# Four slots instead of three for split weights in a two-block transformer kernel, with half the space for dynamic descriptors

## What is computed

```python
x = x + hybrid_mixer(rms_norm(x, norm_mix_g), w_in, ...)
x = x + memory_cross_attention(rms_norm(x, norm_xa_g), mem, ...)
x = x + swiglu(rms_norm(x, norm_ffn_g), w_gate_ffn, w_up_ffn, w_down_ffn)
x = rms_norm(x, final_g)
...
x = x + _mixer(_rms(x, norm_mix_g), lb, w_in, b_in, ..., out_g, w_out)
x = x + _conv_glu(_rms(x, norm_ffn_g), w_up, ffn_conv_w, ffn_conv_b, w_down)
```

## Time and profile before

| | value |
|---|---|
| median of three executions | 1623.43 us |
| the profiled execution, its own time | 1622.02 us |
| its span, first to last instruction | 1620.3 us |
| instructions in it | 23388 |
| VectorE busy | 1084.5 us (67%) |
| ScalarE busy | 804.8 us (50%) |
| GpSimd busy | 145.7 us (9%) |
| read from memory, written | 284.58 MB, 96.50 MB |

### The profile page before, as it was taken

One profiled execution on the slowest core, in us unless ns is written; L12 is line 12 of the kernel. 1 busy time (PEld: TensorE's weight loads), 2 busy tenths in 40 slices (PEclk: granted clock), 3 DMA queues, 4 the chain that ended last, 5 costly groups with the idle time before them and its releaser, 6 DMA issues. The chain is left out here.

```text
span 1620.3 us, 23388 instructions
## 1 busy us (share of the span) xinstructions
PE 1608.4 (99%) x9266; PEld 1368.5 (84%) x9266; DVE 1084.5 (67%) x1592; ACT 804.8 (50%) x1242; POOL 145.7 (9%) x173
## 2 busy tenths in 40 slices
PE   9999999999999999999999999999999999999999
PEld 7788878888888779999999977777767788998889
DVE  5346755555564458886886897667555688867886
ACT  5344333332454347654654665257674455544453
POOL 0001001122210001000000020312111200000000
PEclk9999999999999999999999999999999999999999
DMA  7653985968756954555557749531213564463235
GB/s 296 245 186 104 245 261 180 324 251 220 231 178 215 242 149 142 185 179 184 183 181 239 248 155 246 183 136 54 66 65 117 150 200 141 119 201 106 87 87 185
DMA packets 83644, 290.32 MB, mean 179 GB/s; under 512 B 9472, under 2 KB 11648, under 8 KB 76560
## 3 DMA queue, kind: packets, MB, share of 16 engines
q1 hardware_dynamic: 76464, 238.46, 42.9%
q0 software_dynamic: 6784, 49.84, 14.6%
q10 hardware_dynamic: 288, 0.54, 0.1%
HBM read 284.58 MB, written 96.50 MB: 235 GB/s over the span
## 5 line engine op out<-in xcount | busy, mean ns | idle before, releaser
L2042 DVE TENSOR_TENSOR WL<-raw,WH 128x1024 fp32r<-128x1024 f32 (+2 forms) x358 | 420.9, 1177 | 206.3 <-ACT WH L1260 195.1
L1260 ACT ACTIVATE WH<-raw 128x1024 fp32r<-128x1024 f32 (+3 forms) x360 | 361.0, 1005 | 250.1 <-PE pst L576 243.3
L576 PE MATMUL pst<-XH,WH 128*128 128x512 f32 x960 | 385.9, 402 | 1.0 <-DVE XL L2054 0.6
L576 PE MATMUL pst<-XH,WL 128*128 128x512 f32 x960 | 374.4, 390 | 0.0
L576 PE MATMUL pst<-XL,WH 128*128 128x512 f32 x960 | 374.0, 390 | 0.0
L576 PEld LDWEIGHTS pst<-XH,WH 128*128 128x128 f32 x960 | 180.2, 188 | 49.0 <-issue 11.5
L576 PEld LDWEIGHTS pst<-XH,WL 128*128 128x128 f32 x960 | 180.2, 188 | 38.5
L576 PEld LDWEIGHTS pst<-XL,WH 128*128 128x128 f32 x960 | 180.4, 188 | 38.0 <-issue 2.6
L576 PE MATMUL pst<-XCH,WH 128*128 128x256 f32 x616 | 174.6, 283 | 0.3 <-ACT pst L1260 0.2
L576 PE MATMUL pst<-XCL,WH 128*128 128x256 f32 x616 | 174.3, 283 | 0.0
L576 PE MATMUL pst<-XCH,WL 128*128 128x256 f32 x616 | 174.3, 283 | 0.0
(11 more groups left out here) (314 smaller groups left out, 2385.5 us busy)
## 6 DMA issues: line engine op xcount, KB each, us to landing
raw<-wst SPq DMA_DIRECT2D x191, 512.0 KB, 4.0
raw<-sums SPq DMA_DIRECT2D x120, 256.0 KB, 2.9
sums<-wup POOLq DMA_DIRECT2D x8, 2816.0 KB, 35.7
sums<-sums SPq DMA_DIRECT2D x32, 704.0 KB, 6.2
sums<-wd POOLq DMA_DIRECT2D x8, 2816.0 KB, 19.5
raw<-wup SPq DMA_DIRECT2D x66, 256.0 KB, 2.9
sums<-wup SPq DMA_DIRECT2D x16, 704.0 KB, 5.5
sums<-wd SPq DMA_DIRECT2D x16, 704.0 KB, 10.8
```

Source lines behind the costliest of these rows:

```text
L576: return nc.tensor.matmul(out, lhs, rhs, start=start, stop=stop, skip_group_check=more)
L1260: return nc.scalar.activation(out, in_, func, **kw)
L2042: vec.tensor_tensor(WL[:, i % NHL, 0:n], raw[:, i % NRAW, 0:n], WH[:, i % NHL, 0:n].bitcast(F32), ALU.subtract).then_inc(wl, 1)
```

## The change

```diff
@@ -20,7 +20,7 @@
 CH = 8
 NRAW = 5
 WARM = 12
-NHL = 3
+NHL = 4
 NEG = -1.0e30
 EPS = 1e-6
@@ -3396,7 +3396,7 @@
-    nc = bacc.Bacc("TRN2", target_bir_lowering=False, num_devices=1)
+    nc = bacc.Bacc("TRN2", target_bir_lowering=False, num_devices=1, dynamic_dma_scratch_size=8192)
```

## The result

| | before | changed |
|---|---|---|
| median of 5 runs, us | 1623.37 | 1633.09 |
| lowest to highest | 1622.13 to 1624.02 | 1631.60 to 1634.50 |
| profiled execution, its time | 1622.02 | 1632.71 |
| its span | 1620.3 | 1631.0 |
| mean granted clock of the TensorE | 0.999 | 0.996 |

The changed kernel is slower: ratio 1.0062 with an interval of 1.0050 to 1.0075, that is 9.7 us. The forecast was 1623.0 us and its range ended at 1627.0, so this is a miss.

A forecast was written before the change was run, and what follows sets the result against it. The TensorE, busy 1608.4 of 1620.3 us, was taken as the bound. Terms -0.4 + 0.1 - 0.2 + 0.1, the rest 0, gave -0.4 us: 1621.6 profiled, 1623.0 as median, range 1619.8 to 1627.0.

The forecast's parts named there:

- What bounds the kernel, and what the change does to the waits: Whole kernel: TensorE is the limit; awaited counts stay, so ScalarE's 243.3 us stay and only waits on WL can shrink.
- the faster rival: Whole kernel: slots were the limit, so the TensorE's waits shrink by 6.3 us, to 1617.1 us; chance 0.05.
- Part 1: TensorE's three waits on WL, 0.8 us, placed in the first network's last products: -0.4 us taken, plus 0.1 and -0.2.
- the extra width: Norm chain after the first network: a 1024-wide split replaces a 768-wide one, up to +0.3 us, +0.1 taken.
- Part 2: Start of the kernel: ScalarE's third split ahead of ZH runs in idle time; cost 0.
- Part 3: Second mixer, loads behind the store of X: late landing makes ScalarE wait 9.7 us, costing the TensorE 0.1; bounds 0 and 9.7.
- What is queued behind: Second mixer: ScalarE's exponentials and ucol 2 to 3 us late; VectorE's half of the second split ends near 1048.9.
- the cover is just used up: Second mixer near 1051.3, TensorE's sum of squares of X: ScalarE's 9.7 us of waits cost the TensorE only 0.1.
- 310.20 us: A like place for a late load, expected in time or 1 to 2 us late; bounds 0 and 3.0, 0 taken.
- Part 4: Four large dynamic transfers from 154.01: half the descriptor space still holds them; cost 0.
- The load wait reaches the TensorE: Split at 1036.93, decided by the second load landing after 1046.6: 1628.3 us, or 1636 at worst; chance 0.09.
- a wait of over 1 us on the TensorE between 1043 and 1060: Second mixer: a sign that would make the forecast wrong, as would GpSimd's issues spreading over 20 us.

The follow-up runs named there:

- the loads ahead: The changed kernel with three more loads, of chunks 238 to 240, issued ahead of the store of X: 1622.12 us, ratio 1.0002.
- the two that move chunk 238: The changed kernel with chunk 238's split one call later, on ScalarE and VectorE: 1622.26 us, ratio 1.0000; on VectorE only: 1622.63 us, ratio 1.0004.
- three-slot kernel: The kernel before, three slots and full space, with one load fewer (chunk 237) ahead of the store of X: 1630.83 us, ratio 1.0050.
- three splits held: Four slots, three more loads ahead of the store of X, splits of chunks 226, 254 and 262 one call later: 1623.38 us, ratio 1.0008.

## Why the prediction was wrong

**What bounds the kernel, and what the change does to the waits: right.** The awaited counts are the same, and ScalarE's waits for a slot stayed at 240.5 us of 243.3. The slots weren't the limit. With the loss taken away, four slots give a ratio of 1.0002 (0.9992 to 1.0011), which leaves out the 6.3 us of the faster rival.

**Part 1, the waits on WL: the row went as forecast, the term has the wrong sign.** The row is gone, and the wait for TL rose from 1.2 to 1.9 us. The step took half of the 0.8 us to stay and 0.1 for the extra width, -0.3 in all. It put all three waits at the end of the first network. Two of them, 0.4 us, stand there. The third stands in the second network of the kernel before, where nothing takes the gain back:

```profile
1282.78 0.47 PE L576 MATMUL pst<-XH,WH 128*128 128x512 f32 x1 [0.38 <-DVE WL L2042]
```

At the first place all that was gained went, and more. Between the same two TensorE instructions, at 930.1 and 972.98 in the kernel before, the four kernels with four slots and no split held there (the changed one, the loads ahead, and the two that move chunk 238) take 43.9 us, and the four kernels with three slots 42.9: a loss of 1.1 us. At 1282.78 each of the four gains 0.5. By these two places the term is about +0.5, outside the bounds that the step gave (-0.8 and +0.3). The spread of the runs is wider than that.

**Part 2, the extra split at the start: right.** ZH starts at 30.80 us where it started at 30.95.

**Part 3, a load that hasn't landed: the step that failed.** The right chunk, the right place in ScalarE's stream and the right wait were named: 6.5 us expected, 6.38 measured in the three-slot kernel and 8.39 in the changed one, where the load took 11.64 us and the store stood 0.8 us later. The total of waits on loads, 14.7 us for "some 15", agrees by luck: the first wait was 2 us longer than forecast, and the second, of "some 2 us", didn't come. What failed is the next sentence, "What is queued behind". It lists ScalarE's exponentials and ucol, and follows VectorE only for its half of the **second** split. VectorE's half of the **first** was left out. That one stands directly ahead of lines 2904 and 2905, whose sums the TensorE used 0.25 us after they were ready. So "the cover is just used up" was said of a place with cover, while 10 us earlier on another engine there was next to none. For the path that the step did follow, 0.1 us was not far off: with ScalarE alone late by 7.5 us the TensorE waited 0.7 us.

The right working from rows of the kernel before: the load lands at 1043.4 instead of in time for 1036.9. ScalarE's half, VectorE's half and the two additions take 1.04 + 1.2 + 0.8 us behind it, so the TensorE goes on at about 1046.5 instead of 1040.15. That is 6.3 us, and 1629.7 us in all. The three-slot kernel with one load late is this case: its TensorE lost 6.3 us at this place. Its loss of 8.8 us in all is larger by the clock's share. The bounds of the part, 0 to 9.7 us, held the 8.3 us that the TensorE lost at this place, but not the clock's share, which comes on top.

**What no term held: the clock.** A bottleneck that stands 6.1 or 8.1 us goes on at the lower level for about 5 us, and this cost 2.3 us after the longer stop and 2.2 after the shorter. The rest of the distance is the landing, 11.6 us instead of 9.7. The TensorE's 8.3 at the wait, 2.3 for the clock, and the 0.8 that it was behind before, less the 0.7 regained later, give the 10.7 us between the spans.

**310.20 us: right.** ScalarE's split there has no wait for its load.

**Part 4, the space: right.** 1622.3 us with the space alone, beside 1622.0.

**The rivals.** "The load wait reaches the TensorE" was the right one, with too small a chance, 0.09, and for a reason that doesn't hold: it was tied to the landing of the second load, as if only a late copy could decide it. The place that decides was the first split, and there the wait was certain from the order of instructions and a landing time already read. It had 1636 us only with a mishap at 310.20 added; the price that VectorE's stream gives for a landing in 9.7 us is 1629.7, and 1631.9 with the clock's 2.2. The rest of the measured 1633.09 is in the main the later landing. What was to show the forecast wrong, "a wait of over 1 us on the TensorE between 1043 and 1060", came at 1049.28.

## What to carry to other kernels

A wait that is put into an in-order stream is paid by everything behind it on that engine, and when a step is computed in halves on two engines, each half has its own queue behind it. List for every engine that takes part the next instruction that the bottleneck needs, and its room: here 0.25 us on VectorE and some 7 us on ScalarE. A deeper prefetch whose compute runs one step further ahead needs loads that go out one step earlier too. If a store or another wait holds the loads back in their queue, the prefetch moves a wait for memory forward into the path. The cost of each of the two stops of the TensorE was more than its length: add what its clock takes to come back.

## What the runs showed of the hardware that was not expected

After a stop of 8.1 us the granted clock was 0.58 over the next 5.7 us, and after one of 6.1 us it was 0.54 over 5.0 us. They cost 2.3 and 2.2 us, so the price hardly grew with the length of the stop. The clock also falls behind a short wait, in some executions. Around the wait of 2.3 us for YYL, in a stretch that the TensorE fills thinly, three kernels with the same matmuls have, first the kernel before, then the one with four slots and the loads ahead of the store, then the one with three splits held:

```profile
1214.00:1218.00 4.00, 3.65 (x9) 2.49 (x10) 4.00 (x5) 3.98 (x8) 1.77 (x2) 0.57 0.00 1
```

```profile
1214.00:1218.00 4.00, 2.14 (x8) 1.45 (x9) 3.71 (x5) 4.00 (x8) 2.88 (x3) 1.00 0.00 0
```

```profile
1219.00:1224.00 5.00, 5.00 (x16) 3.91 (x15) 4.94 (x7) 4.34 (x7) 0.45 (x1) 0.60 0.59 212
```

The clock is at its lower level for most of the stretch in the first, at the upper in the second, and low behind the wait in the third, the slowest of the held versions. Of the ten kept profiles eight show such a fall at this place, and two keep the upper level (the second above, and the kernel with three slots and one load late). From the end of the wait for YYL to the same product some 11 us on, these two take 10.3 us each, the other eight 11.1 to 12.4. It goes with a good part of the 3 us by which runs of the same kernel differ: of the 33 runs of the kernel before on the second chip, the four with a mean granted clock of 1.000 took 1620.5 to 1621.1 us, the 25 with 0.999 took 1620.8 to 1622.7, and the four with 0.998 took 1623.1 to 1623.7. What decides which of these an execution meets was not settled.

What stays open: why the first load behind the store of 2048 KB took 11.64 us in the changed kernel and 9.7 us before. The number of slots doesn't decide it. This is the landing of that load with three slots and half the space, then in the changed kernel with chunk 238 split later on both engines:

```profile
DMA to landing us min/median/max: 11.7/11.7/11.7
```

```profile
DMA to landing us min/median/max: 9.9/9.9/9.9
```

With the split later on VectorE only it is 10.8. So the four kernels with half the space have 9.9 to 11.7 us, and the two with the full space in which this load goes out behind the store 9.6 and 9.7, in one profile each. That the smaller space has a share in the later landing, and so in up to 2 us of the loss, is neither shown nor ruled out: the kernel with the space alone has cover at this place, and four slots with the full space were not tried.
